# S5 coefficients, matrices and scan as separate units in the planned order of a hybrid decoder step

## The reference

```python
lam_bar = jnp.exp(lam * dt)
b_bar = ((lam_bar - 1.0) / lam)[:, :, None] * b_c
bu = jnp.einsum('gph,bsgh->bsgp', b_bar, uf.astype(jnp.complex64))
...
a_cum, h = lax.associative_scan(combine, (a, bu), axis=1)
h = h + a_cum * h0[:, None]
y = jnp.real(jnp.einsum('ghp,bsgp->bsgh', c_c, h))
...
y = jax.nn.gelu(y.reshape(nb, ns, S5_WIDTH))
y = y * jax.nn.sigmoid(y @ w_glu.astype(jnp.float32) + b_glu.astype(jnp.float32))
```

## Time and profile before

| | |
|---|---|
| median of 3 runs | 1459.25 us (1457.52 to 1462.02) |
| the profiled execution | 1464.86 us, its span 1463.1 us |
| TensorE busy | 1279.2 us, 87% of the span |
| VectorE busy | 521.6 us, 36% |
| ScalarE, GpSimd busy | 248.5 us, 214.7 us |
| moved by DMA | 458.31 MB, mean 313 GB/s |
| cached pages | 512 + 512 loads of 256 KB, median 4.7 us from issue to landing |

### The profile page before, as it was taken

The page is one execution under the profiler, slowest core; times in us unless marked ns, Lnnn a source line. Parts: engine busy times, 40 slices in busy tenths (PEclk is TensorE's granted clock), DMA queues, the critical chain, the costliest instruction groups (busy, mean ns, idle before and its releaser), DMA issues.

```text
span 1463.1 us, 26568 instructions
## 1 busy us (share of the span) xinstructions
PE 1279.2 (87%) x9000; PEld 670.6 (46%) x9000; DVE 521.6 (36%) x1413; ACT 248.5 (17%) x476; POOL 214.7 (15%) x329
## 2 busy tenths in 40 slices
PE   7999999999869799998869999976899999999930
PEld 4545555554324346666544444433444444444410
DVE  2723543253365455553512111153122111121126
ACT  2101111121212233332212000000011111111111
POOL 2003140313100200000010000001122222222211
PEclk9999999999989999998999999976999999999975
DMA  9989998869968999999996998998899999999764
GB/s 364 329 310 293 321 294 283 272 198 298 298 227 304 352 338 363 365 315 323 331 387 228 330 336 293 322 349 321 277 324 371 360 354 363 361 363 366 256 211 179
DMA packets 185201, 458.31 MB, mean 313 GB/s; under 512 B 23953, under 2 KB 24337, under 8 KB 176530
## 3 DMA queue, kind: packets, MB, share of 16 engines
q1 hardware_dynamic: 163602, 390.21, 75.4%
q0 software_dynamic: 21504, 66.78, 13.8%
HBM read 421.92 MB, written 33.80 MB: 311 GB/s over the span
## 4 chain that ended last, share of the span: by engine, by line
PE 70%; DMA 12%; DVE 7%; SPq 5%; issue 3%; DVEq 2%; ACT 1%; POOL 0%; ACTq 0%; POOLq 0%
PE WA L1800 52%; PE SC L1800 7%; PE OD L1800 7%; DMA ring<-in_cacheK 6%; SPq L500 4%; DMA qpad<-h_scratch,idc 3%; DMA ring<-in_cacheV 2%; PE WA L2166 2%; DVE arena L1769 1%; PE WA L1919 1%; DVE arena L1782 1%; DVE st L1141 1%; PE WA L2126 1%; DMA arena<-y_scratch 1%; DVEq L1771 1%
## 5 line engine op out<-in xcount | busy, mean ns | idle before, releaser
L1800 PE MATMUL WA<-arena 128*128 128x512 f32 (+10 forms) x1440 | 353.4, 432 | 17.6 <-issue 7.2
L1800 PE MATMUL WA<-arena,xm 128*128 128x512 f32 (+3 forms) x816 | 313.6, 581 | 8.4 <-DMA arena<-in_w_out 6.5
L1800 PEld LDWEIGHTS WA<-arena 128*128 128x128 f32 (+2 forms) x1440 | 191.6, 195 | 155.0 <-issue 135.5
L1800 PEld LDWEIGHTS WA<-arena,xm 128*128 128x128 f32 (+1 forms) x816 | 124.4, 174 | 162.8 <-issue 154.7
L1800 PE MATMUL WA<-xm,arena 128*128 128x512 f32 x192 | 87.3, 603 | 1.7 <-ACT arena L958 1.3
L1800 PE MATMUL OD<-ring,sall 128*32 128x512 f32 x512 | 71.0, 670 | 15.0 <-DMA ring<-in_cacheV 15.0
L563 POOL TENSOR_TENSOR st<-st,consts 128x1 f32<-128x1 f32 (+2 forms) x18 | 13.8, 765 | 466.2 <-DVEq L1175 280.0
L1800 PE MATMUL OD<-ring,qpad 128*32 128x128 f32 x2048 | 67.9, 285 | 15.7 <-DMA ring<-in_cacheK 15.7
L1800 PEld LDWEIGHTS OD<-ring,qpad 128*32 128x32 f32 x2048 | 56.6, 114 | 35.9 <-DMA ring<-in_cacheK 18.4
L1800 PE MATMUL SC<-ring,qpad 128*32 128x128 f32 x2048 | 64.9, 278 | 9.1 <-DMA ring<-in_cacheK 9.0
L1712 DVE TENSOR_TENSOR xm<-WA,colw 128x960 f32<-128x960 f32 x16 | 18.5, 1158 | 147.2 <-PE WA L2166 147.2
(11 more groups left out here) (364 smaller groups left out, 1244.1 us busy)
## 6 DMA issues: line engine op xcount, KB each, us to landing
ring<-in_cacheK SPq DMA_DIRECT2D x512, 256.0 KB, 4.7
ring<-in_cacheV SPq DMA_DIRECT2D x512, 256.0 KB, 4.7
arena<-in_w_gu SPq DMA_DIRECT2D x16, 2048.0 KB, 9.8
arena<-in_w_dn SPq DMA_DIRECT2D x16, 1024.0 KB, 14.3
ring<-in_w_gu SPq DMA_DIRECT2D x8, 2048.0 KB, 10.3
xm<-in_w_gu SPq DMA_DIRECT2D x8, 2048.0 KB, 10.5
ring<-in_w_dn SPq DMA_DIRECT2D x8, 1024.0 KB, 14.8
xm<-in_w_dn SPq DMA_DIRECT2D x8, 1024.0 KB, 14.8
```

The costliest lines, as they stand in the source:

```text
L1800: return pe.matmul(out, lhsT, rhs, start=first, stop=last, **kw)
```

## The change

`s5a` becomes four units (cut behind the first waits for ScalarE, behind the input matrix, and within the table of powers), `bA(n)` two and `bH(n)` three: (n,0) the multiplication by the table, (n,1) the recurrences, (n,2) the rest. Every instruction is the same as before, and so are the waits; each part keeps its place within its own stream, but units of other streams can stand between two parts. ScalarE's and GpSimd's share stays whole and goes with one of the parts. The lags are the old ones, divided: 10 us between parts of `s5a` and 12 behind it, 4.5 between those of `bA`, 4.2, 3.4 and 6.2 along `bH`; `bP` and `bK` follow `bA(n,0)` by the old 5 and 11. The costs and the planner are untouched.

```diff
@@ -140,14 +140,16 @@
-    s5 = [(("s5a",), 0.0, [(("dprep",), 2.0)])]
+    s5 = [(("s5a", 0), 0.0, [(("dprep",), 2.0)])] + [(("s5a", p), 0.0, [(("s5a", p - 1), 10.0)]) for p in range(1, 4)]
     for n in range(NQ):
-        x = [(("bY", n - 1, 1), 0)] if n else [(("u", 3, 1, 1), 4.0), (("dk2",), 3.0), (("s5a",), 60.0)]
-        s5 += [(("bU", n), 0.0, x + [(("u", n, 1, 1), 3.0)]), (("bA", n), 0.0, x), (("bP", n), 1.1, [(("bA", n), 5.0)]),
-               (("bK", n), 2.1, [(("bA", n), 11.0)]), (("bE", n), 0.0, [(("bK", n), 2.5)])]
+        x = [(("bY", n - 1, 1), 0)] if n else [(("u", 3, 1, 1), 4.0), (("dk2",), 3.0), (("s5a", 3), 12.0)]
+        s5 += [(("bU", n), 0.0, x + [(("u", n, 1, 1), 3.0)]), (("bA", n, 0), 0.0, x), (("bA", n, 1), 0.0, [(("bA", n, 0), 4.5)]),
+               (("bP", n), 1.1, [(("bA", n, 0), 5.0)]),
+               (("bK", n), 2.1, [(("bA", n, 0), 11.0)]), (("bE", n), 0.0, [(("bK", n), 2.5)])]
         s5 += [(("bX", n, j), 0.75, [(("bP", n), 2.2), (("bU", n), 14.0)]) for j in range(JQ)]
-        s5 += [(("bH", n), 0.0, [(("bX", n, JQ - 1), 1.2)])]
-        s5 += [(("bY", n, 0), 3.5, [(("bH", n), 13.5), (("bK", n), 13.0)]), (("bG", n, 0), 0.0, [(("bY", n, 0), 2.0)]),
+        s5 += [(("bH", n, 0), 0.0, [(("bX", n, JQ - 1), 1.2)]), (("bH", n, 1), 0.0, [(("bH", n, 0), 4.2)]),
+               (("bH", n, 2), 0.0, [(("bH", n, 1), 3.4)])]
+        s5 += [(("bY", n, 0), 3.5, [(("bH", n, 2), 6.2), (("bK", n), 13.0)]), (("bG", n, 0), 0.0, [(("bY", n, 0), 2.0)]),
...
@@ -632,7 +634,9 @@
-            def bH(n):
+            def bH(n, p):
+                if p < 2:
+                    return
                 gp.wait_ge(s_scan, n + 1)
...
@@ -872,9 +876,12 @@
-            def s5a():
-                act.wait_ge(s_ld5, 32)
-                act.activation(sm5[:, 0, :], par[:, 2, :], ACT.Exp).then_inc(s_act5, 1)
+            def s5a(p):
+                if p == 0:
+                    act.wait_ge(s_ld5, 32)
+                    act.activation(sm5[:, 0, :], par[:, 2, :], ACT.Exp).then_inc(s_act5, 1)
+                if p != 1:
+                    return
                 act.wait_ge(s_dve5, 1)
...
@@ -1263,7 +1270,7 @@
-            def s5a():
+            def s5a_parts():
...
                 dve.drain().then_inc(s_dve5, 1)
+                yield
                 dve.wait_ge(s_act5, 4)
...
+                yield
                 a, b = (v[7], v[6]), (v[18], v[19])
...
                     a, b = b, a
...
+                    if tab is T1 and k == 4:
+                        yield
+                yield
+
+            s5a_part = s5a_parts()
+
+            def s5a(p):
+                next(s5a_part)
...
+            def bA(n, p):
...
+                if p == 0:
...
+                    dve.drain().then_inc(s_pA, 1)
+                    return
                 for m in range(2):
                     dve.tensor_copy(Bt[:, m, :, :, :], bc[:, 0, m, j, :].unsqueeze(2).to_broadcast(full))
...
-            def bH(n):
+            def bH(n, p):
...
+                if p == 0:
+                    dve.wait_ge(s_Xs, JQ * (n + 1))
...
+                    dve.drain()
+                    return
+                if p == 1:
+                    for j in range(JQ):
...
+                    dve.drain()
+                    return
                 dve.tensor_tensor(X[0], A, Er, MUL)
```

45 lines of the change are left out of this document (20 added, 25 removed).

## The result

| | before | after |
|---|---|---|
| median | 1460.63 us (1457.12 to 1466.50, 6 runs) | 1480.05 us (1475.00 to 1485.64, 6 runs) |
| ratio, 95% interval | | 1.0133 [1.0102, 1.0164] |
| profiled execution: span, granted clock | 1463.1 us, 0.94 | 1478.3 us, 0.931 |

The change costs 19 us (15 to 24). The forecast was +3.6 us and its range ended at 1473, so the measured time lies outside it. The page after shows the same work: the columns of its first part are busy us, share of the span and instructions.

A forecast was written before the change was run, and what follows sets the result against it. TensorE was taken to set the pace ahead of the expert stage, with one large VectorE wait. -14.3 + 10.0 + 3.7 + 2.0 + 1.5 - 1.2 + 1.9 = +3.6 us on 1459.25 gave 1462.9 us, range 1450 to 1473.

The forecast's parts named there:

- The removed waits, -14.3 us: Attention-weight transposes' three waits for VectorE, 11.1 us of them at once behind the fourth scan block, would go: -14.3 us.
- Rival 4: The ring evens it out: shorter waits for VectorE become longer waits for pages; 1459 us, no change; chance 0.11.
- ot(1), 8.8 us: Output transposes wait 8.8 us behind the scan's last part and AN(1); with two combinations, 10.0 us new.
- bP(3), T(0), bK: Divided matrices: 2.0 us wait at bP(3) and 1.7 at the transposes, 3.7 new; bK(1), bK(2) add 2.0.
- Tiles 3 to 5: Attention tiles where whole units change places: ot(3), ot(4) lose 2.7 us of waits, ot(5) gains 1.5; -1.2 us.
- The clock, 0 in the sum: Half-speed stretch behind the long wait: nothing given back, as the new wait is nearly as long.
- The end, +1.9 us: Stage end: three V groups behind the list matmuls instead of two, output products ending 3.9 us earlier; +1.9 us.
- Rival 2: The page stream decides the end: two additional groups cost 6.1 us each, +8.3 instead of +1.9; 1469 us; chance 0.20.
- s5a: Dividing the coefficients gives and costs nothing, value 0; a mishap would cost 1 to 2 us.
- three at +7.4: Clock case: three new waits as long as the old one would make the sum +7.4 us instead of +3.6.
- three things I said would prove me wrong: ot(1) under 3 us; VectorE waits 380-500 us falling over 8; last V group over 6 us off the sum.
- both bad ends at once: Case left outside the range, whose top of 1473 us was set above rival 2.

The follow-up runs named there:

- coef_mats_only: Kernel before with only coefficients s5a and matrices bA divided, the scan whole: 1464.44 us, ratio 0.9992 [0.9960, 1.0024].
- norms_first: Kernel before, on VectorE the fourth scan in three parts behind C(1,0), C(1,1), AN(0), and AN(3) to AN(6) right behind O(i,3): 1459.32 us, ratio 0.9990.
- two_groups_behind: both_moved with one V group moved from behind the list matmuls to ahead of them, leaving two behind: 1461.28 us, ratio 1.0004 against the kernel before.
- mid_after_end_before: Changed order up to transposes hT(0), order of the kernel before behind them: 1478.86 us, ratio 1.0090 [1.0058, 1.0123] against the kernel before.
- both_moved: Changed kernel, on VectorE bH(3,2) moved behind C(2,1) and AN(2) behind O(2,3): 1469.48 us, ratio 1.0051 against the kernel before.

## Why the prediction was wrong, point by point

- **The removed waits, -14.3 us: the step that failed first.** I took the three waits of T at their face. The runs give 2.6 us [-2.3, 7.6] and 5.4 us [1.0, 9.6] for the large one, since 5.5 and 6.1 us of wait for VectorE remain and since, as I argue, pages limit TensorE from ot(1) to ot(2). Rival 4, which I gave 0.11, comes nearest for this term, though it names pages alone. My argument against it, that the DMA engines ran dry in the wait, spoke of that stretch and not of the one behind it, where their share is 0.99 (477.5 to 513.2 us before). Besides, T still waits 9.0 us in the changed kernel; 5.1 of them, from 516 us on, stand in no term.
- **ot(1), 8.8 us: right** in mechanism and size, 9.82 us; bH(3,2) is ahead of AN(1) with 5.5 us as worked out.
- **ot(2) was not in the sum at all.** Its 4.27 us come from AN(2) standing behind the maxima of S(3,0) and S(3,1). Before, it stood between the two. That is only a change of place of whole units, like those of tiles 3 to 5 that I did follow; I had not checked tile 2. Moving AN(2) brought 6.7 us, uncertain by 7; adding such a wait to the kernel before cost 6.1 us [2.6, 9.8].
- **bP(3), T(0), bK: right or close.** bP(3) waits 2.96 us (2.0 forecast), T 1.56 and 0.58 (1.7), bK(1) 1.94 (2.3), bK(2) 0.94 (1.0), bK(0), which I had left out, 1.71; ot(0) 3.27 against 1.5. By coef_mats_only what the division of the matrices costs in the old order can't be told from nothing.
- **Tiles 3 to 5:** ot(3) waits no more and ot(5) waits 1.61 us (1.5 forecast), but ot(4) still waits 1.71 us, not zero. norms_first takes most of such waits away and wins nothing that can be measured.
- **The clock, 0 in the sum: the second failed step.** I let old and new wait cancel, since they are nearly equally long. But the old wait stood ahead of two half products and V groups, and TensorE was at full clock again from 436 on; behind ot(2) come matmuls of 128 and 136 columns and V groups, with more waits among them, and it stayed at half clock for 20 us. The Trainium skill (TensorE: Matmul & The Clock Gate, section "HAM oscillation — how this bites in real kernels") says that a kernel whose array idles again and again pays each time; the traces agree, with TensorE busy for 1291.3 us in the changed kernel against 1279.2 before, for the same matmuls. I had written that by this page the number of long waits matters, and priced three at +7.4; the price was too small and I did not let it into the sum.
- **The end, +1.9 us: right mechanism, probably too small.** Measured 5.7 us [1.8, 9.6]; the changed kernel's trace has 11.8 us from the last output product to the end where I had 5.8. I let the third group's pages arrive 6 us behind the first use of the ring; they are asked for from 1004.25 on and used at 1013.46, 9.2 us later and 11.4 us behind the first use. Rival 2 named the number of groups left as the cause at 6.1 us each; two_groups_behind refutes that. It is the one group more than the ring holds.
- **s5a: nothing speaks against it.** TensorE has no wait over 0.2 us from 75 to 125 us in the changed kernel; it was divided together with the matrices only (coef_mats_only, 0.9992 [0.9960, 1.0024]).

My sum of waits for VectorE in the middle was +1.7 us; they rose by 16.8 (24.4 to 41.2 in mid_after_end_before). Of the three things I said would prove me wrong, the last one came true: the end of the V groups is 15.6 us later than before in the table, where the sum had put it 3.6 later. The range failed since I varied its terms one by one and left "both bad ends at once" outside. But even rival 2's +8.3 and the clock's +3.8 together bring my sum only to +13.8, below the interval of what was measured. The larger part is the removed waits, +9 to +12: with 2.6 to 5.4 in place of 14.3, 6.7 for ot(2) and 5.7 for the end (timed, so with the clock in them) my sum becomes +23 to +26 against 19.4 measured, an estimate of which each part is uncertain by 4 to 8 us.

## What to carry to other kernels

When a planned order puts work of a second engine at cost zero, follow *every* place where the first engine waits for it, also where only whole units have changed places; the edited units are not the only ones whose neighbours change. Look at what stands behind a wait: behind one of 11.13 us, ahead of half products, TensorE was at full clock again after 7 us; behind one of 4.27 us, ahead of smaller matmuls with further waits, only after 20. Before counting a removed wait as a gain, look at the next 50 us: if the DMA engines are at 0.98 there, or the second engine has hardly a gap, the gain may be held up there. A kernel joined from two plans can have a loss of its own at the joint; look at its trace before reading its time as a part of the whole. With a prefetch ring of two groups, leave no more than two groups behind any long stretch that uses none.

## What the runs showed of the hardware that I had not expected

Matmuls of 128 and 136 columns and V groups can run at 1.2 GHz for 20 us with TensorE busy 9.80 and 7.88 of 10 us (500 to 520 us of the changed kernel), while behind a wait of 11.13 us, with half products following, the granted clock was 0.68 from 429 to 436 us and 1.00 from 436 to 440.

The mean granted clock goes along with the time, also between runs of one kernel: over 131 runs of the kernel before the fastest (1450.49 us) had 0.948 and one of 1471.90 us 0.933; the correlation is -0.85, with 10.7 us for 0.01 of clock. The kernels' medians follow: 0.940 before, 0.930 after, 0.935 in both_moved. That is no proof of cause, but the 12 us of added busy time of the changed kernel with the same matmuls fit it, and it is why differences under 0.3% could not be told here.

Eight page loads of 256 KB took 4.38 us to be issued on SyncE's queue, 0.51 to 0.58 us apart for the first seven. The half group used at 1013.46 needs the first four, issued by 1006.12; the fourth landed at 1013.42. So 1.9 of the 9.2 us from the request to the use are issuing, and 7.6 the flight of the fourth page, against a median of 4.7 us.
